# One semaphore per part of a weight unit, and matrix products with the upper part first

## Chip, cores and metric

The kernel runs on 1 core of one Trainium2 chip. The metric is the device time of one launch in microseconds (us); less is better. Three runs of the kernel before took 3330.92, 3332.18 and 3332.82 us; the median is 3332.18 us. TensorE is called PE below, VectorE DVE, ScalarE ACT, GpSimd POOL and SyncE SP.

## The reference

One inference step of a four-layer decoder, for a prompt of 512 tokens and 8 samples of 8 tokens: 576 tokens of width 1024. Layers 0 and 3 mix tokens with a gated MLP (gMLP), layer 1 with a convolution module, layer 2 with latent attention (MLA). Each layer ends in a SwiGLU of inner width 2816:

```
for i in range(DEPTH):                      # 4
    kind = i % 3                            # gMLP, convolution, MLA
    hp = xp * (1 + sc1p) + sh1p             # and the same for the samples
    op = gmlp_mixer(hp, ...) or conv_module(hp, ...) or mla(...)
    xp = layer_norm(ALPHA * xp + g1p * op, ln_mix_g[i], ln_mix_b[i])
    fp = (silu(h2 @ w_gate) * (h2 @ w_up)) @ w_down      # h2 = xp * (1 + sc2p) + sh2p
    xp = layer_norm(ALPHA * xp + g2p * fp, ln_ffn_g[i], ln_ffn_b[i])
```

All inputs are float32. The shifts, scales and gates come from a product of the condition vector with `ada_w`, 24 MB of weights for a layer.

## The kernel before

**Split operands.** Every weight and activation is split into an upper part (rounded to the matmul's reduced type, `w_hi`, `h_hi`, `a_hi`) and a lower part, the remainder (`w_lo`, `h_lo`, `a_lo`). For each block of 128 contracted values (an index k) PE computes three products into one PSUM bank: upper times upper, upper weight times lower activation, lower weight times upper activation.

**Units.** Weights come in units of up to 128 x 1024 values, 416 of them. There are five slots (`SLOTS`), unit u lies in slot u % 5. SP loads a unit into `w_raw`, which has the same memory as `w_lo` (`load_to`, L598), once PE has finished the last product with the unit five before it (a count of `acc_ready`). POOL makes `w_hi` from it (L717), then `w_lo` in place (L719), and counts up `split_full` once (`split_to`). SP also loads the `ada_w` blocks of 1 MB, in the same queue (L617).

**PE's order** is written out by hand. `take_units(k)` waits until the next k units are split as a whole, and hands out their slots. `half_product` is one unit of 128 output columns by one half of the tokens (288): 8 values of k, 24 matmuls (6 values of k and 18 matmuls in some units). In `gate_up` a step takes two units, one of the gate and one of the up matrix, and makes four such products. Each result is taken out of its bank by ACT and DVE, which then count up `acc_free`.

**After each LayerNorm** the next stage starts with `first_four`: four banks, first with k 0 to 3 (part 0), then with k 4 to 7 (part 1), since DVE delivers the lower part of the activations (`h_lo`, L2005) in quarters, counted by `h_ready`. In `first_halves` (gate_up and convolution) the four banks belong to four units, which are taken two at a time, at bank 0 and at bank 2; in `first_tokens` (gMLP and MLA) the activations are the stationary operand, and bank 2 takes the second pair of units. After bank 0 of part 1 PE makes the sums of the second token half for the LayerNorm, with `ones` as weights (`second_stats`; it waits for DVE's partial sums, L1947 and L1952, by `part_ready`); DVE and ACT then need them for the second half of `h_lo`, which the second call of `first_four` waits for.

**The matmuls of one product, before:**

```
for e, (w, a) in enumerate(((wh, ah), (wh, al), (wl, ah))):
    last = mm(out, lhsT, rhs, q == 0 and e == 0, q == n - 1 and e == 2)
```

The functions that the change touches, with what calls them:

Of the kernel before, what the change touches and what calls it, by code (L numbers as in the profile page):

```python
# [99 lines left out]
def trunk(nc, A, O):  # L100
    ctx = ExitStack()
    with ctx:
        def sem(name):
            return ctx.enter_context(nc.semaphore(name))
# [193 lines left out]
        act_c = sem("act_c")  # L298
        split_full = sem("split_full")
        acc_ready = sem("acc_ready")  # L300
# [408 lines left out]
        def _(pool):  # L709
            DG = Tally()  # L710

            def split_to(end):
                while U.n < end:
                    u = U.n
                    s, w = u % SLOTS, plan.words[u]
                    pool.wait_ge(raw_full[s], landed[u])
                    nc.gpsimd.tensor_scalar(w_hi[:, s, 0:w], w_raw[:, s, 0:w], 1.0, 1.0, ALU.mult, ALU.mult)  # L717
                    pool.drain()  # L718
                    nc.gpsimd.tensor_tensor(w_lo[:, s, 0:w], w_raw[:, s, 0:w], w_hi[:, s, 0:w].bitcast(F32),  # L719
                                            ALU.subtract).then_inc(split_full, 1)  # L720
                    U.up()
# [55 lines left out]
        def _(pe):  # L777
# [64 lines left out]
            def half_product(slot, kt, h, act, waits=None, a_waits=None):  # L842

                b = acc_bank()
                hi, lo = act
                if waits is not None or a_waits is not None:
                    for k in range(kt):
                        if k % 4 == 0 and a_waits is None:
                            pe.wait_ge(h_ready, 4 * waits + 2 * h + k // 4 + 1)
                        elif k % 4 == 0:  # L850
                            pe.wait_ge(a_ready, 8 + a_waits + 8 * h + k + 4)
                        for e, (w, a) in enumerate(((w_hi, hi), (w_hi, lo), (w_lo, hi))):
                            last = mm(pb[:, b, 0:HALF], w[:, slot, k * P:(k + 1) * P], a[:, k, half_cols(h)],
                                      k == 0 and e == 0, k == kt - 1 and e == 2)
# [15 lines left out]
            def late_product(s, kt, late):  # L870


                b = acc_bank()
                for k in range(kt):
                    if k in (0, kt - late):
                        pe.wait_ge(a_ready, 8 + AR.n - 2 * (late if k == 0 else 0))
                    for e, (w, a) in enumerate(((w_hi, a_hi), (w_hi, a_lo), (w_lo, a_hi))):
                        last = mm(pb[:, b, 0:HALF], w[:, s, k * P:(k + 1) * P], a[:, k, 0:HALF],
                                  k == 0 and e == 0, k == kt - 1 and e == 2)
                last.then_inc(acc_ready, 1)  # L880
                G.up()
# [39 lines left out]
            def first_four(t, h, step, units=None):  # L921
# [3 lines left out]
                for part_ in range(2):  # L925
                    pe.wait_ge(h_ready, 4 * t + 2 * h + part_ + 1)
                    for i in range(4):
                        if part_ == 0:
                            if units is not None and i % 2 == 0:
                                units(i // 2)  # L930
                            pe.wait_ge(acc_free, G.n + i + 1)
                        for k in range(4 * part_, 4 * part_ + 4):
                            last = step(i, k, (G.n + i) % BANKS)
                        if part_:
# [17 lines left out]
            def first_tokens(t, h, slots, widths):  # L952


                def step(i, k, b):
                    blk, tt = ((0, 2), (0, 3), (0, 4), (1, 2))[i] if h else divmod(i, 2)
                    n = widths[blk]
                    s, c = slots[blk][k // 4], slice(k % 4 * n, (k % 4 + 1) * n)
                    for e, (w, a) in enumerate(((w_hi, h_hi), (w_hi, h_lo), (w_lo, h_hi))):
                        last = mm(pb[:, b, 0:n], a[:, k, token_tile(tt)], w[:, s, c], k == 0 and e == 0,  # L960
                                  k == KT - 1 and e == 2)
                    return last

# [18 lines left out]
            def down_norm(kt, turn=False, by_half=False, late=0, between=None):  # L982

                slots = []
                if by_half and between is None:
                    for part_ in range(2):
                        pe.wait_ge(a_ready, 8 + AR.n - 16 + 4 * part_ + 4)
                        for i in range(4):
                            if part_ == 0:
                                slots += take_units(1)  # L990
                                pe.wait_ge(acc_free, G.n + i + 1)
                            for k in range(4 * part_, 4 * part_ + 4):
                                for e, (w, a) in enumerate(((w_hi, a_hi), (w_hi, a_lo), (w_lo, a_hi))):
                                    last = mm(pb[:, (G.n + i) % BANKS, 0:HALF], w[:, slots[i], k * P:(k + 1) * P],
                                              a[:, k, 0:HALF], k == 0 and e == 0, k == KT - 1 and e == 2)
                            if part_:
# [29 lines left out]
                b = acc_bank()  # L1026
                for k in range(kt):
                    for e, (w, a) in enumerate(((w_hi, a_hi), (w_hi, a_lo), (w_lo, a_hi))):
                        last = mm(pb[:, b, 0:HALF], w[:, slots[0], k * P:(k + 1) * P], a[:, k, half_cols(1)],
                                  k == 0 and e == 0, k == kt - 1 and e == 2)  # L1030
                    if k == kt // 2 - 1:
                        pe.wait_ge(part_ready, PT.n + 3)
# [1613 lines left out]
```

## Time and profile before

| quantity | value |
|---|---|
| median of three runs | 3332.18 us |
| the profiled execution's own time | 3332.91 us |
| its span | 3331.1 us |
| PE busy with matmuls | 3136.7 us (94%), 22524 matmuls |
| DVE busy | 1602.5 us (48%) |
| POOL busy | 1528.2 us (46%) |
| moved by DMA, mean | 104 GB/s |
| granted clock of PE, mean over the span | 0.974 |

The span runs from the first to the last instruction; the time of an execution is some 2 us more. A granted clock of 1.00 means 2.4 GHz for PE and 0.50 means 1.2 GHz. A matmul's row shows its length with what overlaps the next one, about 290 ns; the step from one start to the next is what counts. In a timeline the brackets at the end of a row give the idle time of the engine before it, and what ended it.

### The profile page before, as it was taken

To read this page: it belongs to the slowest core of one execution; us is meant where nothing else is said; L and a number is where in the kernel's file an instruction comes from. 1 tells how busy PE (TensorE), PEld (TensorE's weight loads), DVE (VectorE), ACT (ScalarE), POOL (GpSimd) and SP (SyncE) were. 2 spreads that over 40 slices of the span, in tenths; PEclk is the share of its full clock that TensorE was granted. 3 is DMA by queue.
4 is the path that set the end of the run, shared out by engine and by line. 5 is a ranking of instruction groups with operands and counts; after the bars stand their busy time and mean duration, and the time that the engine had idled before them with its cause. 6 is when DMAs were issued, how large, how long until landed. Compare 5 with 4: busy or idle time off the path is not lost.

```text
span 3331.1 us, 54036 instructions
## 1 busy us (share of the span) xinstructions
PE 3136.7 (94%) x22524; PEld 2898.7 (87%) x22524; DVE 1602.5 (48%) x2621; ACT 544.3 (16%) x1114; POOL 1528.2 (46%) x880
## 2 busy tenths in 40 slices
PE   6999999999899799999989888999999999899997
PEld 5999989999876589999986568999998999899997
DVE  3163563423688763424556536342353435634245
ACT  3120130000310240000233214000023201400002
POOL 2354445545467445455520044555553554455551
PEclk8999999999999899999989999999999999999998
DMA  5542344442221144433221324443222232122221
GB/s 218 213 119 72 111 173 129 140 130 80 80 64 39 31 170 128 152 126 96 79 69 43 109 79 152 133 152 118 89 77 71 79 95 80 58 83 83 83 85 52
DMA packets 450784, 344.83 MB, mean 104 GB/s; under 512 B 24953, under 2 KB 435953, under 8 KB 438238
## 3 DMA queue, kind: packets, MB, share of 16 engines
q1 hardware_dynamic: 441616, 323.89, 31.0%
q10 hardware_dynamic: 8925, 17.51, 1.5%
q8 instruction: 178, 2.92, 0.4%
q14 instruction: 65, 0.52, 0.0%
HBM read 336.81 MB, written 5.25 MB: 103 GB/s over the span
## 4 chain that ended last, share of the span: by engine, by line
issue 38%; POOL 24%; PE 19%; POOLq 11%; DVE 6%; DVEq 1%; ACT 1%; DMA 0%; ACTq 0%
POOL w_lo L719 24%; PE pb L789 18%; POOLq L718 11%; DVE pb L2263 2%; DVE pgT L2503 0%; DVE full L2247 0%; DVE yc L2272 0%; DVE xa L1978 0%; DVE att L2461 0%; DVE full L2249 0%; DVE pb L1971 0%; PE pb L866 0%; DMA out_y_prompt<-yo 0%; POOL a_lo L770 0%; DVEq L1977 0%
## 5 line engine op out<-in xcount | busy, mean ns | idle before, releaser
L717 POOL TENSOR_SCALAR w_hi<-w_raw 128x1024 fp32r<-128x1024 f32 (+2 forms) x416 | 448.4, 1078 | 1472.5 <-DMA w_raw<-in_ffn_w_up 423.1
L789 PE MATMUL pb<-h_hi,w_hi 128*128 128x288 f32 x3584 | 1074.0, 300 | 47.9 <-DVE h_lo L2005 21.8
L789 PE MATMUL pb<-h_lo,w_hi 128*128 128x288 f32 x3584 | 1061.7, 296 | 0.0
L789 PE MATMUL pb<-h_hi,w_lo 128*128 128x288 f32 x3584 | 1061.7, 296 | 0.0
L719 POOL TENSOR_TENSOR w_lo<-w_raw,w_hi 128x1024 fp32r<-128x1024 f32 (+2 forms) x416 | 985.1, 2368 | 62.1 <-issue 1.3
L789 PEld LDWEIGHTS pb<-h_hi,w_hi 128*128 128x128 f32 x3584 | 678.4, 189 | 102.0 <-issue 47.2
L789 PE MATMUL pb<-a_hi,w_hi 128*128 128x288 f32 x2176 | 652.3, 300 | 33.1 <-DVEq L2192 16.2
L789 PEld LDWEIGHTS pb<-h_lo,w_hi 128*128 128x128 f32 x3584 | 678.7, 189 | 0.3
L789 PEld LDWEIGHTS pb<-h_hi,w_lo 128*128 128x128 f32 x3584 | 678.5, 189 | 0.0
L789 PE MATMUL pb<-a_hi,w_lo 128*128 128x288 f32 x2176 | 646.4, 297 | 0.0
L789 PE MATMUL pb<-a_lo,w_hi 128*128 128x288 f32 x2176 | 646.3, 297 | 0.0
L789 PEld LDWEIGHTS pb<-a_hi,w_hi 128*128 128x128 f32 x2176 | 413.8, 190 | 41.7 <-DVEq L2192 17.1
L789 PEld LDWEIGHTS pb<-a_lo,w_hi 128*128 128x128 f32 x2176 | 413.5, 190 | 0.8
L789 PEld LDWEIGHTS pb<-a_hi,w_lo 128*128 128x128 f32 x2176 | 413.5, 190 | 0.0
L2079 DVE TENSOR_TENSOR pr<-pb,sg 128x288 f32<-128x288 f32 x176 | 80.2, 458 | 647.4 <-PE pb L789 646.7
L1553 ACT ACTIVATE sg<-pb 128x288 f32<-128x288 f32 x176 | 72.1, 411 | 1391.1 <-PE pb L789 1391.1
L1833 DVE TENSOR_TENSOR a_lo<-pr,a_hi 128x288 fp32r<-128x288 f32 x176 | 258.8, 1471 | 14.0 <-issue 1.1
L789 PE MATMUL pb<-w_hi,h_hi 128*128 128x256 f32 (+1 forms) x760 | 220.5, 290 | 28.9 <-DVE h_lo L2005 20.0
L1937 DVE SCALAR_TENSOR_TENSOR xa<-pb,gate,xa 128x288 f32<-128x288 f32 (+1 forms) x288 | 137.9, 480 | 208.5 <-PE pb L789 207.2
L789 PE MATMUL pb<-w_hi,h_lo 128*128 128x256 f32 (+1 forms) x760 | 217.4, 286 | 0.0
L789 PE MATMUL pb<-w_lo,h_hi 128*128 128x256 f32 (+1 forms) x760 | 217.1, 286 | 0.0
L789 PEld LDWEIGHTS pb<-w_hi,h_hi 128*128 128x128 f32 x760 | 148.7, 196 | 36.1 <-DVE h_lo L2005 21.7
(280 smaller groups left out, 2989.8 us busy)
## 6 DMA issues: line engine op xcount, KB each, us to landing
ada_w<-in_ada_w SPq DMA_DIRECT2D x88, 1024.0 KB, 5.8
w_raw<-in_ffn_w_gate SPq DMA_DIRECT2D x88, 512.0 KB, 4.5
w_raw<-in_ffn_w_up SPq DMA_DIRECT2D x88, 512.0 KB, 3.7
w_raw<-in_gmlp_w_in SPq DMA_DIRECT2D x64, 512.0 KB, 4.4
w_raw<-in_ffn_w_down SPq DMA_DIRECT2D x64, 512.0 KB, 4.0
w_raw<-in_gmlp_w_out SPq DMA_DIRECT2D x32, 512.0 KB, 4.2
w_raw<-in_ffn_w_down SPq DMA_DIRECT2D x32, 384.0 KB, 3.4
w_raw<-in_conv_w_pw SPq DMA_DIRECT2D x24, 512.0 KB, 3.9
```

The lines of the kernel that those rows point to most:

```text
L717: nc.gpsimd.tensor_scalar(w_hi[:, s, 0:w], w_raw[:, s, 0:w], 1.0, 1.0, ALU.mult, ALU.mult)
L718: pool.drain()
L719: nc.gpsimd.tensor_tensor(w_lo[:, s, 0:w], w_raw[:, s, 0:w], w_hi[:, s, 0:w].bitcast(F32), ALU.subtract).then_inc(split_full, 1)
L789: return nc.tensor.matmul(out, lhsT, rhs, start=start, stop=stop)
L1553: fn(sg[:, q, :], pb[:, b, 0:HALF], func, **kw).then_inc(sg_ready, 1)
L1833: return v.tensor_tensor(lo, src, hi.bitcast(F32), ALU.subtract)
L1937: last_ = v.scalar_tensor_tensor(out=y, in0=ps[:, 0:w], scalar=gp, in1=y, op0=ALU.mult, op1=ALU.add)
L2079: v.tensor_tensor(pr[:, q, :], pb[:, (G.n + 1) % BANKS, 0:HALF], sg[:, q, :], ALU.mult).then_inc(acc_free, 2)
L2263: v.scalar_tensor_tensor(out=own if k < CW - 1 else yp, in0=full[:, m % 3, k:k + SEQ], scalar=one(wdT, m, slice(k, k + 1)), in1=own, op0=A ...
```

## The change

POOL counts up `split_hi` when the upper part of a unit is written, and `split_lo` when the lower part is. `take_units` waits for nothing any more; PE waits for `split_hi` of a unit in front of the first matmul that reads its upper part, and for `split_lo` in front of the first that reads its lower part. In a product (or in a part of four values of k, where a product was cut before) the matmuls with the upper part come first, two for each k, and then those with the lower part, one for each k. The number of matmuls is the same, and so are the waits for activations and banks and the points at which products are reported as done.

```
-        split_full = sem("split_full")
+        split_hi = sem("split_hi")
+        split_lo = sem("split_lo")
...
                     pool.wait_ge(raw_full[s], landed[u])
-                    nc.gpsimd.tensor_scalar(w_hi[:, s, 0:w], w_raw[:, s, 0:w], 1.0, 1.0, ALU.mult, ALU.mult)
+                    nc.gpsimd.tensor_scalar(w_hi[:, s, 0:w], w_raw[:, s, 0:w], 1.0, 1.0, ALU.mult, ALU.mult
+                                            ).then_inc(split_hi, 1)
                     pool.drain()
                     nc.gpsimd.tensor_tensor(w_lo[:, s, 0:w], w_raw[:, s, 0:w], w_hi[:, s, 0:w].bitcast(F32),
-                                            ALU.subtract).then_inc(split_full, 1)
+                                            ALU.subtract).then_inc(split_lo, 1)
...
             def take_units(k):
-                pe.wait_ge(split_full, U.n + k)
                 slots = [(U.n + n) % SLOTS for n in range(k)]
+                for n, s in enumerate(slots):
+                    unit_in[s] = U.n + n
                 U.up(k)
                 return slots
+            unit_in = {}
+            HI, LO = Tally(), Tally()
+            def wait_hi(s):
+                if unit_in[s] >= HI.n:
+                    HI.up(unit_in[s] + 1 - HI.n)
+                    pe.wait_ge(split_hi, HI.n)
+            def wait_lo(s):
+                if unit_in[s] >= LO.n:
+                    LO.up(unit_in[s] + 1 - LO.n)
+                    pe.wait_ge(split_lo, LO.n)
...
             def product(out, ks, w_at, m_hi, m_lo, w_moves=False):
-                n = len(ks)
+                return part_product(out, ks, w_at, m_hi, m_lo, True, True, w_moves)
+            def part_product(out, ks, w_at, m_hi, m_lo, first, end, w_moves=False):
                 for q, k in enumerate(ks):
                     s, cols = w_at(k)
-                    wh, wl = w_hi[:, s, cols], w_lo[:, s, cols]
-                    ah, al = m_hi(k), m_lo(k)
-                    for e, (w, a) in enumerate(((wh, ah), (wh, al), (wl, ah))):
-                        lhsT, rhs = (a, w) if w_moves else (w, a)
-                        last = mm(out, lhsT, rhs, q == 0 and e == 0, q == n - 1 and e == 2)
+                    wait_hi(s)
+                    for e, a in enumerate((m_hi(k), m_lo(k))):
+                        lhsT, rhs = (a, w_hi[:, s, cols]) if w_moves else (w_hi[:, s, cols], a)
+                        mm(out, lhsT, rhs, first and q == 0 and e == 0, False)
+                for q, k in enumerate(ks):
+                    s, cols = w_at(k)
+                    wait_lo(s)
+                    lhsT, rhs = (m_hi(k), w_lo[:, s, cols]) if w_moves else (w_lo[:, s, cols], m_hi(k))
+                    last = mm(out, lhsT, rhs, False, end and q == len(ks) - 1)
                 return last
...
             def first_halves(t, h, slots):
-                def step(i, k, b):
-                    s, c = slots[i], slice(k * P, (k + 1) * P)
-                    for e, (w, a) in enumerate(((w_hi, h_hi), (w_hi, h_lo), (w_lo, h_hi))):
-                        last = mm(pb[:, b, 0:HALF], w[:, s, c], a[:, k, half_cols(h)], k == 0 and e == 0,
-                                  k == KT - 1 and e == 2)
-                    return last
+                def step(i, ks, b):
+                    return part_product(pb[:, b, 0:HALF], ks, lambda k: (slots[i], slice(k * P, (k + 1) * P)),
+                                        lambda k: h_hi[:, k, half_cols(h)], lambda k: h_lo[:, k, half_cols(h)],
+                                        0 in ks, KT - 1 in ks)
                 first_four(t, h, step, None if h else lambda _: slots.extend(take_units(2)))
...
```

The other places that had their own loop of three matmuls (`half_product`, `late_product`, `first_tokens`, `down_norm`) call `part_product` in the same way.

In the program before, PE, at the third bank of the very first `first_four` (layer 0, gMLP; `w_hi` and `w_lo` move, `h_hi` and `h_lo` are stationary, waits in brackets):

```order
L789 MATMUL pb<-w_hi,h_lo 128x256
L789 MATMUL pb<-w_lo,h_hi 128x256
L789 MATMUL pb<-w_hi,h_hi 128x256 [waits acc_free,split_full]
L789 MATMUL pb<-w_hi,h_lo 128x256
L789 MATMUL pb<-w_lo,h_hi 128x256
L789 MATMUL pb<-w_hi,h_hi 128x256
```

One wait for both units of the pair stands ahead of all matmuls of bank 2. At the same place in the program after, from the end of bank 1 through bank 2:

```order
L810 MATMUL pb<-w_lo,h_hi 128x256 x4
L810 MATMUL pb<-w_hi,h_hi 128x256 [waits split_hi,acc_free]
L810 MATMUL pb<-w_hi,h_lo 128x256
L810 MATMUL pb<-w_hi,h_hi 128x256
L810 MATMUL pb<-w_hi,h_lo 128x256
L810 MATMUL pb<-w_hi,h_hi 128x256
L810 MATMUL pb<-w_hi,h_lo 128x256
L810 MATMUL pb<-w_hi,h_hi 128x256
L810 MATMUL pb<-w_hi,h_lo 128x256
L810 MATMUL pb<-w_lo,h_hi 128x256 [waits split_lo]
L810 MATMUL pb<-w_lo,h_hi 128x256 x3
```

Bank 2 now begins behind a wait for the upper part of one unit, and its lower part is waited for eight matmuls later; the second unit of the pair is not asked for until part 1.

Before, PE, at the first step of `gate_up` behind the two calls of `first_four` (layer 0):

```order
L789 MATMUL pb<-h_hi,w_hi 128x288
L789 MATMUL pb<-h_lo,w_hi 128x288
L789 MATMUL pb<-h_hi,w_lo 128x288
L789 MATMUL pb<-h_hi,w_hi 128x288 [waits acc_free,split_full]
L789 MATMUL pb<-h_lo,w_hi 128x288
L789 MATMUL pb<-h_hi,w_lo 128x288
```

The wait in the fourth row is for two units, the gate's and the up matrix's. In the program after, further down in the same step, where the gate's product passes to its lower part and the up matrix's product begins:

```order
L810 MATMUL pb<-h_hi,w_hi 128x288
L810 MATMUL pb<-h_lo,w_hi 128x288
L810 MATMUL pb<-h_hi,w_lo 128x288 [waits split_lo]
L810 MATMUL pb<-h_hi,w_lo 128x288 x7
L810 MATMUL pb<-h_hi,w_hi 128x288 [waits split_hi,acc_free]
L810 MATMUL pb<-h_lo,w_hi 128x288
```

The gate's lower part is waited for behind 16 matmuls of its product, and the up matrix's unit behind all 24.

## Rows read from the trace of the kernel before

**Rows 1.** The page: span, and busy time of each engine.

```profile
span 3331.1 us, 54036 instructions
PE 3136.7 (94%) x22524; PEld 2898.7 (87%) x22524; DVE 1602.5 (48%) x2621; ACT 544.3 (16%) x1114; POOL 1528.2 (46%) x880
```

**Rows 2.** Waits of PE: line waited for, us in total, times, longest.

```profile
PE pb L789 <- POOL w_lo L719: 27.1, 14, 3.6
```

**Rows 3.** Timeline of PE: start, duration (us), instruction, count, idle before.

```profile
48.07 0.28 PE L789 MATMUL pb<-w_lo,h_hi 128*128 128x256 f32 x1
51.98 0.58 PE L789 MATMUL pb<-w_hi,h_hi 128*128 128x256 f32 x1 [3.64 <-POOL w_lo L719]
...
429.74 0.40 PE L789 MATMUL pb<-h_hi,w_hi 128*128 128x288 f32 x1 [1.43 <-POOL w_lo L719]
...
464.18 0.40 PE L789 MATMUL pb<-h_hi,w_hi 128*128 128x288 f32 x1 [2.67 <-POOL w_lo L719]
464.42 0.30 PE L789 MATMUL pb<-h_lo,w_hi 128*128 128x288 f32 x1
...
1031.01 0.40 PE L789 MATMUL pb<-h_hi,w_hi 128*128 128x288 f32 x1 [1.81 <-POOL w_lo L719]
...
1233.82 0.40 PE L789 MATMUL pb<-h_hi,w_hi 128*128 128x288 f32 x1 [2.80 <-POOL w_lo L719]
...
2061.82 0.61 PE L789 MATMUL pb<-h_hi,w_hi 128*128 128x288 f32 x1 [3.04 <-POOL w_lo L719]
...
2531.24 0.39 PE L789 MATMUL pb<-w_hi,h_hi 128*128 128x256 f32 x1 [0.27 <-POOL w_lo L719]
...
2899.11 0.40 PE L789 MATMUL pb<-h_hi,w_hi 128*128 128x288 f32 x1 [2.63 <-POOL w_lo L719]
```

**Rows 4.** Windows: length, busy (x matmuls) of PE, PEld, DVE, ACT, POOL; PEclk, DMA.

```profile
51.90:57.10 5.20, 5.12 (x24) 5.12 (x25) 4.55 (x4) 3.48 (x6) 3.59 (x3) 0.50 0.00 2
...
464.10:469.00 4.90, 4.82 (x36) 4.82 (x37) 0.65 (x2) 4.90 (x10) 0.03 (x1) 1.00 1.04 388
1234.80:1238.00 3.20, 3.20 (x15) 3.20 (x14) 0.00 (x0) 3.20 (x7) 0.00 (x0) 0.50 1.02 379
...
2061.80:2067.30 5.50, 5.47 (x23) 5.48 (x24) 0.60 (x2) 4.19 (x9) 0.00 (x0) 0.50 1.05 372
2900.50:2903.70 3.20, 3.20 (x15) 3.20 (x14) 0.00 (x0) 3.19 (x7) 3.19 (x2) 0.50 0.09 26
```

**Rows 5.** Timeline of POOL, at the start and at two places of layer 0.

```profile
44.94 2.38 POOL L719 TENSOR_TENSOR w_lo<-w_raw,w_hi 128x1024 fp32r<-128x1024 f32 x1
...
49.58 2.35 POOL L719 TENSOR_TENSOR w_lo<-w_raw,w_hi 128x1024 fp32r<-128x1024 f32 x1
...
427.31 2.37 POOL L719 TENSOR_TENSOR w_lo<-w_raw,w_hi 128x1024 fp32r<-128x1024 f32 x1
...
460.58 1.06 POOL L717 TENSOR_SCALAR w_hi<-w_raw 128x1024 fp32r<-128x1024 f32 x1 [26.01 <-DMA w_raw<-in_ffn_w_up]
461.78 2.35 POOL L719 TENSOR_TENSOR w_lo<-w_raw,w_hi 128x1024 fp32r<-128x1024 f32 x1
```

**Rows 6.** Windows: the longest stretch of PE without a stall (layer 3).

```profile
2955.25:3280.60 325.35, 325.35 (x2455) 325.35 (x2456) 1.00 0.28 82
```

**Rows 7.** Timeline of DVE at the start: second and third quarter of `h_lo`.

```profile
46.68 1.85 DVE L2005 TENSOR_TENSOR h_lo<-hf,h_hi 128x1152 fp32r<-128x1152 f32 x1 [2.79 <-ACT h_hi L1519]
...
53.74 3.11 DVE L2005 TENSOR_TENSOR h_lo<-hf,h_hi 128x1152 fp32r<-128x1152 f32 x1 [0.48 <-issue]
```

**Rows 8.** Windows: the convolution loop behind PE's stall at 1031.01.

```profile
1031.00:1060.00 29.00, 28.88 (x163) 22.77 (x164) 26.46 (x34) 2.37 (x4) 24.20 (x11) 1.00 0.13 38
```

**Rows 9.** Timeline behind LayerNorm (layer 0): DVE's sums, PE's sums, PE's next wait.

```profile
433.00 2.24 DVE L1952 TENSOR_REDUCE part<-sq 128x288 f32<-128x1152 f32 x1
...
434.58 2.10 PE L789 MATMUL pb<-part,ones 128*128 128x288 f32 x8
447.67 0.41 PE L789 MATMUL pb<-h_hi,w_hi 128*128 128x288 f32 x1 [2.68 <-DVE h_lo L2005]
```

More of the change, by code:

```diff
@@ L846, in half_product @@
                 if waits is not None or a_waits is not None:
-                    for k in range(kt):
-                        if k % 4 == 0 and a_waits is None:
+                    for k in range(0, kt, 4):
+                        if a_waits is None:
                             pe.wait_ge(h_ready, 4 * waits + 2 * h + k // 4 + 1)
-                        elif k % 4 == 0:
+                        else:
                             pe.wait_ge(a_ready, 8 + a_waits + 8 * h + k + 4)
-                        for e, (w, a) in enumerate(((w_hi, hi), (w_hi, lo), (w_lo, hi))):
-                            last = mm(pb[:, b, 0:HALF], w[:, slot, k * P:(k + 1) * P], a[:, k, half_cols(h)],
-                                      k == 0 and e == 0, k == kt - 1 and e == 2)
+                        last = part_product(pb[:, b, 0:HALF], range(k, min(k + 4, kt)),
+                                            lambda k: (slot, slice(k * P, (k + 1) * P)),
+                                            lambda k: hi[:, k, half_cols(h)], lambda k: lo[:, k, half_cols(h)],
+                                            k == 0, k + 4 >= kt)
                 else:
@@ L873, in late_product @@
                 b = acc_bank()
[L874 to L879, printed above, removed]
+                for k0, k1 in ((0, kt - late), (kt - late, kt)):
+                    pe.wait_ge(a_ready, 8 + AR.n - 2 * (kt - k1))
+                    last = part_product(pb[:, b, 0:HALF], range(k0, k1), lambda k: (s, slice(k * P, (k + 1) * P)),
+                                        lambda k: a_hi[:, k, 0:HALF], lambda k: a_lo[:, k, 0:HALF], k0 == 0, k1 == kt)
                 last.then_inc(acc_ready, 1)
@@ L931, in first_four @@
                             pe.wait_ge(acc_free, G.n + i + 1)
-                        for k in range(4 * part_, 4 * part_ + 4):
-                            last = step(i, k, (G.n + i) % BANKS)
+                        last = step(i, range(4 * part_, 4 * part_ + 4), (G.n + i) % BANKS)
                         if part_:
@@ L940, in first_halves, with step @@
             def first_halves(t, h, slots):
[L943 to L948 removed]
+                def step(i, ks, b):
+                    return part_product(pb[:, b, 0:HALF], ks, lambda k: (slots[i], slice(k * P, (k + 1) * P)),
+                                        lambda k: h_hi[:, k, half_cols(h)], lambda k: h_lo[:, k, half_cols(h)],
+                                        0 in ks, KT - 1 in ks)
                 first_four(t, h, step, None if h else lambda _: slots.extend(take_units(2)))
             def first_tokens(t, h, slots, widths):
[L955 removed]
+                def step(i, ks, b):
                     blk, tt = ((0, 2), (0, 3), (0, 4), (1, 2))[i] if h else divmod(i, 2)
                     n = widths[blk]
[L958 to L962, printed above, removed]
+                    return part_product(pb[:, b, 0:n], ks,
+                                        lambda k: (slots[blk][k // 4], slice(k % 4 * n, (k % 4 + 1) * n)),
+                                        lambda k: h_hi[:, k, token_tile(tt)], lambda k: h_lo[:, k, token_tile(tt)],
+                                        0 in ks, KT - 1 in ks, w_moves=True)
                 def units(blk):
@@ L991, in down_norm @@
                                 pe.wait_ge(acc_free, G.n + i + 1)
[L992 to L995, printed above, removed]
+                            last = part_product(pb[:, (G.n + i) % BANKS, 0:HALF], range(4 * part_, 4 * part_ + 4),
+                                                lambda k: (slots[i], slice(k * P, (k + 1) * P)),
+                                                lambda k: a_hi[:, k, 0:HALF], lambda k: a_lo[:, k, 0:HALF],
+                                                part_ == 0, part_ == 1)
                             if part_:
@@ L1026, in down_norm @@
                 b = acc_bank()
[L1027 to L1031, printed above, removed]
+                for k0, k1 in ((0, kt // 2), (kt // 2, kt)):
+                    last = part_product(pb[:, b, 0:HALF], range(k0, k1),
+                                        lambda k: (slots[0], slice(k * P, (k + 1) * P)),
+                                        lambda k: a_hi[:, k, half_cols(1)], lambda k: a_lo[:, k, half_cols(1)],
+                                        k0 == 0, k1 == kt)
+                    if k0 == 0:
                         pe.wait_ge(part_ready, PT.n + 3)
```

## The prediction

> **What bounds the kernel now.** I read the page first. PE is busy for 94% of the span, no other engine for more than half [rows 1], so nearly all time is matmuls, and the change removes none. What it can touch is PE's idle time, so the list of waits comes next: PE waited for POOL's `w_lo` 14 times, 27.1 us in all [rows 2]. The change cannot win more than this and what hangs on it. Then the timeline, for each of the 14. They are of two kinds [rows 3]:
>
> - Seven stand at bank 2 of the `first_four` behind a LayerNorm, all of 1.4 to 1.6 us like the one at 429.74 us.
> - Seven stand elsewhere: 3.64 us at the start (51.98), 2.67, 2.80, 3.04 and 2.63 us at the first ordinary step of `gate_up` in the four layers (464.18, 1233.82, 2061.82, 2899.11), 1.81 us in the convolution (1031.01) and 0.27 us in the last gMLP (2531.24).
>
> The windows behind the stalls come last, for the granted clock. Behind the stall at 51.98 PE runs at 0.50 (1.2 GHz), 24 matmuls in 5.20 us. Behind those at 1233.82, 2061.82 and 2899.11 it is at 0.50 too. Behind the one at 464.18 it stays at 1.00 (2.4 GHz) [rows 4].
>
> **Does the wait go, and what is late next?** At `gate_up` the old wait is for two units. The second one is late: POOL starts it at 460.58, has its upper part at 461.64 and its lower part at 464.13 [rows 5], and PE starts at 464.18 [rows 3]. After the change PE asks first for the gate's unit, which POOL finished long before (it was idle for 26.01 us ahead of 460.58). That product has 24 matmuls. An undisturbed matmul of 288 columns takes 325.35 / 2455 = 0.1325 us from start to start [rows 6], so the product takes 3.18 us, from about 461.4 to 464.5. By then both parts of the second unit are there. Nothing is late next: the stall goes whole. The other three have the same code and the same length.
>
> At the start, bank 2 needs both units of its pair now, the second one's lower part being ready at 49.58 + 2.35 = 51.93 us [rows 5]. After, its part 0 needs the first unit alone, ready at 44.94 + 2.38 = 47.32, before PE gets there (48.07 + 0.12). A matmul of 256 columns is an eighth shorter, 0.12 us, so part 0 ends at 48.2 + 24 x 0.12 = 51.1. Part 1 needs the second quarter of `h_lo`, there at 46.68 + 1.85 = 48.53, and takes 48 x 0.12 = 5.8 us, to 56.9. The second call needs the third quarter, there at 53.74 + 3.11 = 56.85 [rows 7]. So PE's whole lead fits, but only just: a later start than this would have been caught by DVE.
>
> **The terms.** A stall costs its idle time and about 0.15 us of the matmul that is running out: 51.98 - 48.07 - 0.12 = 3.79 for a row with 3.64 of idle [rows 3].
>
> - Start: 3.79 us of stall. Behind it 24 matmuls took 5.20 us instead of 24 x 0.12 = 2.88; I take 2.2 us, since the window is a little wider than they are [rows 4].
> - Layer 0, 464.18: 2.67 + 0.15 = 2.8 us; no clock term.
> - Layer 1, 1233.82: 2.95 us, and the half-speed window of 3.20 us. At 0.50 a matmul takes 5.50 / 23 = 0.239 us instead of 0.1325, so 45% of such time is lost: 1.4 us [rows 4].
> - Layer 2, 2061.82: 3.2 us, and 45% of 5.50 = 2.45 us.
> - Layer 3, 2899.11: 2.8 us, and 1.4 us.
> - Last gMLP, 2531.24: 0.4 us.
> - Convolution, 1031.01: 0. Its stall will go, but DVE is busy 26.46 of the next 29.00 us [rows 8]; it is what the loop waits for, and PE's lead is used up there. At most 1.9 us.
> - The seven behind LayerNorms: 0. At 429.74 POOL's last lower part had come at 427.31 + 2.37 = 429.68 [rows 5]; after, PE needs no more than the third unit and starts bank 2 at about 428.2, 1.6 us sooner. But `second_stats` then stands at 433.0 instead of 434.58 and needs DVE's last sum, which ends at 433.00 + 2.24 = 435.24 [rows 9]. Today PE spends these 0.7 us on the sums that it can already make, and is hardly late; then it will wait about 1.5 us. The stall moves by 5 us and comes back. The next wait (447.67, for `h_lo`) hangs on the same sum. At most 7 x 1.6 = 11 us.
>
> Stalls: 3.8 + 2.8 + 2.95 + 3.2 + 2.8 + 0.4 = 15.95 us. Clock: 2.2 + 1.4 + 2.45 + 1.4 = 7.45 us. Together 23.4 us.
>
> **What it adds.** PE has one wait per unit and part in place of one for each `take_units`: 826 matmuls with a split wait instead of 301, 525 more. Most are satisfied long before. What does a satisfied wait cost? The stretch without a stall has 102 products, each with a wait for its bank and every second one with a wait for a unit, and runs at 0.1325 us throughout [rows 6]. The steps between starts inside its products, 0.13 us, leave no room for a cost. The bound above is what a real stall leaves behind: the matmul after it starts 464.42 - 464.18 = 0.24 us later instead of 0.13, so 0.11 us x 525 = 58 us. I take 0, the value of the nearest rows, because those waits sit in the same kind of stream. The trace has no product whose lower parts follow each other; all three kinds of step (same weight, next weight, same activation) stand in that stretch at one pace, so the order of loads should not matter; 1% either way would be 30 us, and I see no reason for it. On POOL the upper part gets an increment; it waited 26 us here, and 0.05 us on 416 units would be hidden.
>
> [...]
>
> [...]
>
> **From the terms to the time.** 3332.91 - 23.4 = 3309.5 us against the profiled execution's own time. The median of the three runs is 0.7 us below it, so 3308.8; I say 3309.
>
> **The rivals.**
>
> 1. *The gain behind LayerNorms is real* (and the convolution's): 23.4 + 11 + 1.9 = 36 us, 3296. It needs DVE's sums to come sooner, and they don't hang on PE there. 7%.
> 2. *The clock takes part back.* The idle 1.5 us before the sums now lies nearer to the long wait for `h_lo`, and half-speed stretches can begin in layers where there are none. Each costs 1.4 to 2.5 us; with the 5.3 us of the clock terms in `gate_up` not won and up to two new stretches, the time is 3314 + 3 = 3317. For it: which stall is followed by half speed looks accidental. 23%.
> 3. *Slower: satisfied waits are not free* when they stand inside a product, in front of a load that would have been fetched ahead. 525 x 0.11 = 58 us less 23.4: 3367. It is slower than before from 0.045 us a wait on. Against it: the pace of the longest stretch [rows 6]. 5%.
> 4. *No change.* DMA is saturated behind the `gate_up` stalls (388 and 379 GB/s, share over 1.00 [rows 4]) so units land no sooner; if PE's lead only makes it wait for the next pair, or if new stalls of like size come up elsewhere, the time is 3326 to 3339. Against it: the next step, too, asks for its two units 3.2 us apart instead of both at its start, and the step in between takes four products, 12.7 us. 8%.
>
> My forecast, all seven stalls but the convolution's gone and the clock terms won within some 7 us, has the remaining 57%.
>
> **Range and chances.** 3298 holds all but the first rival and a lucky clock; 3323 holds the second rival; what lies outside is about two in ten. A difference of 0.2% (6.7 us) is about what a measurement of this kernel can tell from none. Faster by more: 57 + 7 + 23 = 87%. Within: 8%. Slower: 5%.
>
> **What will show it.** PE's list of waits has no lines of 2 to 3 us for `w_lo` or `w_hi` any more; the first `gate_up` step begins within 0.2 us of the last product. In layer 0 at the start PE runs from 44 to about 63 us without a stall, with the clock at 1.00 from 47 on. `part,ones` rows now have an idle time of 1 to 2 us with DVE's L1952 as releaser, seven times, and the wait for `h_lo` is as long as before. DVE's and POOL's busy times are unchanged, and the 288-column step is 0.1325 us. The forecast is wrong if that step has grown, if PE waits for a DMA or `w_hi` in the second step of `gate_up`, or if the share of half-speed time is not smaller by about 17 us.

## The result, and the profile after

| | before | after |
|---|---|---|
| median, 5 runs each | 3332.22 us | 3314.64 us |
| lowest to highest | 3330.92 to 3335.33 | 3313.22 to 3320.63 |
| the profiled execution's own time | 3332.91 us | 3313.4 us |

The ratio is 0.9948, with a 95% interval of 0.9933 to 0.9963: faster by 0.5%. The forecast was 3309 us with a range of 3298 to 3323. The time lies inside the range, 5.6 us above the point.

The page of the profile after, span and busy times, beside [rows 1]:

```profile
span 3311.6 us, 54131 instructions
PE 3124.5 (94%) x22524; PEld 2885.8 (87%) x22524; DVE 1635.9 (49%) x2621; ACT 544.2 (16%) x1114; POOL 1530.1 (46%) x880
```

PE's busy time fell by 12.2 us with the same number of matmuls; fewer of them ran at half speed. DVE's rose by 33.4 us with the same number of instructions, of which `a_lo` makes 28.9 (258.8 to 287.7 us) and the rounding to `a_hi` 5.4 (128.9 to 134.3): something slows DVE down, which the prediction did not have. It had DVE's busy time unchanged.

PE's waits after (engine, line, what it waited for: us in total, times, longest). Lines of stages that did not change are left out:

```profile
PE pb L810 <- DVE h_lo L2032: 44.0, 12, 8.1
...
PE pb L810 <- DVEq L1980: 14.7, 14, 5.3
...
PE pb L810 <- DVE a_lo L1860: 6.6, 6, 1.2
...
PE pb L810 <- DVE bst L2142: 2.1, 1, 2.1
PE pb L810 <- POOL w_lo L721: 2.0, 2, 1.1
```

Of the 27.1 us for `w_lo` [rows 2] 2.0 are left. Four lines took some of it: L1980, DVE's sums behind LayerNorms (7.9 us in 9 waits before), `a_lo` (one wait before, six now), `bst`, which is new, and `h_lo` (41.8 us in 11 waits before).

Four of the places of [rows 3], in the timeline of PE after. None has an idle time in brackets:

```profile
1224.66 0.29 PE L810 MATMUL pb<-h_hi,w_hi 128*128 128x288 f32 x1
...
2047.71 0.29 PE L810 MATMUL pb<-h_hi,w_hi 128*128 128x288 f32 x1
...
2515.26 0.29 PE L810 MATMUL pb<-w_hi,h_hi 128*128 128x256 f32 x1
...
2878.68 0.29 PE L810 MATMUL pb<-h_hi,w_hi 128*128 128x288 f32 x1
```

The windows behind three of them, beside the third, the fourth and the last of [rows 4] (length; busy time and count of PE, PEld, DVE, ACT, POOL; granted clock; DMA share; GB/s):

```profile
1224.60:1230.10 5.50, 5.50 (x44) 5.50 (x43) 3.15 (x3) 5.50 (x12) 2.77 (x2) 1.00 1.02 429
2047.70:2053.20 5.50, 5.50 (x44) 5.50 (x43) 3.26 (x3) 5.50 (x12) 2.83 (x2) 1.00 1.01 423
2878.60:2884.10 5.50, 5.50 (x44) 5.50 (x44) 3.78 (x3) 5.50 (x12) 5.06 (x4) 1.00 0.83 246
```

The clock stays at 1.00 (2.4 GHz): 44 matmuls in the 5.50 us in which 23 ran before.

In layer 0, POOL's rows for the unit that PE had waited for, beside the last two of [rows 5]:

```profile
456.95 1.05 POOL L718 TENSOR_SCALAR w_hi<-w_raw 128x1024 fp32r<-128x1024 f32 x1 [26.19 <-DMA w_raw<-in_ffn_w_up]
458.17 2.50 POOL L721 TENSOR_TENSOR w_lo<-w_raw,w_hi 128x1024 fp32r<-128x1024 f32 x1 [0.16 <-issue]
```

PE works through the gate's product meanwhile, from 457.27 to 460.4, and has the lower part (ready at 460.67) some 2 us before it asks for it, 16 matmuls into the next product. A stretch without a stall, beside [rows 6]:

```profile
3077.00:3222.00 145.00, 145.00 (x1097) 145.00 (x1096) 50.33 (x76) 6.37 (x16) 78.58 (x45) 1.00 0.27 81
```

145.00 / 1097 = 0.1322 us for a step, as before (0.1325).

**A ledger of the lead.** Both programs have the same 22524 matmuls, so the start of the n-th one before, less its start after, says what has been won up to there. Between two steps this lead stays level within some 0.05 us. Each line is the difference of the levels on its two sides, worked out from the two traces:

```
place (start us before)             step of the lead   forecast
start, up to 57.1                   +5.0
start, 63.0: PE waits for a bank    -2.3               net 6.0, measured 2.7
gate_up layer 0, 464.2              +2.92              2.8
gate_up layer 1, 1233.8 and clock   +3.06 +1.54        2.95 +1.4
gate_up layer 2, 2061.8 and clock   +3.19 +2.68        3.2 +2.45
gate_up layer 3, 2899.1 and clock   +2.89 +1.54        2.8 +1.4
last gMLP, 2531                     +0.53              0.4
convolution, 1031.0 to 1136         +2.07 -2.10        0
seven LayerNorms                    +12.15 -10.68      0
five starts of down products        -6.94              not in it
all else, steps of up to 2.2        +4.2               0
end                                 +19.8              23.4
```

Three places make 4.6 us of "all else" (at 252, 1721 and 2802 us before): there PE ran at half speed for 6.8, 13.7 and 6.8 us in the profile before and for 3.4, 6.8 and 3.4 us in that after. In the second profile of the kernel before it was 6.8, 10.2 and 3.4 us, so this part varies from one execution to the next.

**The start.** PE's timeline after, at bank 2 of the first `first_four`, and where its second call begins to need a bank again:

```profile
49.13 0.41 PE L810 MATMUL pb<-w_hi,h_hi 128*128 128x256 f32 x1
...
57.46 0.64 PE L810 MATMUL pb<-w_lo,h_hi 128*128 128x256 f32 x4
60.20 0.36 PE L810 MATMUL pb<-w_hi,h_hi 128*128 128x256 f32 x1 [2.10 <-DVE bst L2142]
```

DVE at the same time, which answers to [rows 7]:

```profile
53.74 3.15 DVE L2032 TENSOR_TENSOR h_lo<-hf,h_hi 128x1152 fp32r<-128x1152 f32 x1 [0.48 <-issue]
56.99 0.43 DVE L2020 TENSOR_TENSOR hf<-xa,cs 128x256 f32<-128x256 f32 x1
57.49 0.42 DVE L2020 TENSOR_TENSOR hf<-hf,cb 128x256 f32<-128x256 f32 x1
57.99 0.29 DVE L2030 CAST h_hi<-hf 128x256 fp32r<-128x256 f32 x1
58.36 1.36 DVE L2032 TENSOR_TENSOR h_lo<-hf,h_hi 128x1152 fp32r<-128x1152 f32 x1
59.63 1.40 DVE L2142 BATCH_NORM_STATS2 bst<-v_sb 128x6 f32<-128x256 f32 x4
```

Bank 2 starts at 49.13, not at 51.98. PE still ran at half speed then (the third figure from the right is its granted clock):

```profile
43.70:49.60 5.90, 5.75 (x27) 5.76 (x28) 3.01 (x3) 5.90 (x13) 5.57 (x4) 0.51 0.03 9
```

Before, half speed ended at 46.9 us, after at 49.5, which cost about 1 us of the lead. In other profiles it ended at 48.3 (before) and at 49.0 and 48.4 us (after), so this differs by execution. Then, behind its products (here at 60.20) PE needs a free bank, and DVE frees it in its statistics (`bst`), which stand in DVE's queue behind the last quarter of the split. PE arrives earlier and waits for the same thing.

**A LayerNorm** (layer 0), the place of [rows 9]: PE, then DVE.

```profile
428.96 1.13 PE L810 MATMUL pb<-part,ones 128*128 128x288 f32 x4
431.34 1.24 PE L810 MATMUL pb<-part,ones 128*128 128x288 f32 x4 [1.24 <-DVEq L1980]
...
443.57 0.40 PE L810 MATMUL pb<-h_hi,w_hi 128*128 128x288 f32 x1 [2.69 <-DVE h_lo L2032]
```

```profile
429.12 2.13 DVE L1979 TENSOR_REDUCE part<-sq 128x288 f32<-128x1152 f32 x1
```

DVE's sum ends at 429.12 + 2.13 = 431.25, and PE takes it at 431.34, after 1.24 us of idle. The wait for `h_lo` is 2.69 us, before it was 2.68. From the end of PE's sums to the end of this wait it is 443.57 - 432.58 = 10.99 us; before it was 447.67 - 436.68 = 10.99 [rows 9].

**The start of a down product** (layer 0). In the profile after, PE, DVE and POOL:

```profile
829.79 0.41 PE L810 MATMUL pb<-a_hi,w_hi 128*128 128x288 f32 x1 [1.12 <-DVE a_lo L1860]
```

```profile
826.16 0.90 DVE L1858 CAST a_hi<-pr 128x288 fp32r<-128x288 f32 x1
827.13 2.61 DVE L1860 TENSOR_TENSOR a_lo<-pr,a_hi 128x288 fp32r<-128x288 f32 x1
```

```profile
825.84 1.05 POOL L718 TENSOR_SCALAR w_hi<-w_raw 128x1024 fp32r<-128x1024 f32 x1 [5.41 <-DMA w_raw<-in_ffn_w_down]
827.05 2.37 POOL L721 TENSOR_TENSOR w_lo<-w_raw,w_hi 128x1024 fp32r<-128x1024 f32 x1 [0.16 <-issue]
```

In the profile before, DVE and POOL at the same place:

```profile
833.38 0.31 DVE L1831 CAST a_hi<-pr 128x288 fp32r<-128x288 f32 x1
833.76 0.46 DVE L1833 TENSOR_TENSOR a_lo<-pr,a_hi 128x288 fp32r<-128x288 f32 x1
```

```profile
833.83 1.30 POOL L717 TENSOR_SCALAR w_hi<-w_raw 128x1024 fp32r<-128x1024 f32 x1 [5.76 <-DMA w_raw<-in_ffn_w_down]
835.28 2.40 POOL L719 TENSOR_TENSOR w_lo<-w_raw,w_hi 128x1024 fp32r<-128x1024 f32 x1
```

The same instruction, `a_lo`, takes 0.46 us before and 2.61 us after. After, POOL's subtraction had begun 0.08 us ahead of it and ended at 829.42; `a_lo` ended at 829.74, 0.32 us later. All 92 `a_lo` of this kind that began within a subtraction of POOL end 0.31 to 0.32 us after it; before the change these were 73. So DVE did not run slower, it stood until POOL was done. Before, the order at this place was the reverse: `a_lo` had begun 0.07 us ahead of POOL's rounding, and the rounding took 1.30 us in place of 1.05. The Trainium skill, page "SBUF — State Buffer" ("Who interferes with whom"), has this rule: a DVE instruction with two inputs in SBUF and a GpSimd instruction that reads SBUF exclude each other, and whichever issues first blocks the other to its end. The trace agrees with it. The rounding to `a_hi` just ahead stood as well: begun within POOL's rounding it took 0.90 us in place of 0.31.

POOL comes sooner because the units land sooner after SP's issue (issues: count, KB, median us to landing). Before, and then after:

```profile
w_raw<-in_ffn_w_down SPq DMA_DIRECT2D x64, 512.0 KB, 4.0
w_raw<-in_gmlp_w_out SPq DMA_DIRECT2D x32, 512.0 KB, 4.2
```

```profile
w_raw<-in_ffn_w_down SPq DMA_DIRECT2D x64, 512.0 KB, 3.4
w_raw<-in_gmlp_w_out SPq DMA_DIRECT2D x32, 512.0 KB, 3.6
```

### The profile page after: what moved, and what is told of

Read it like the earlier page. It is cut to its first block, busy times and chain, and to the rows that moved or that the text cites. A ratio compares the mean times of both kernels' runs of the same rounds, so it can differ in the third digit from the quotient of the medians.

```text
span 3311.6 us, 54131 instructions
## 1 busy us (share of the span) xinstructions
PE 3124.5 (94%) x22524; PEld 2885.8 (87%) x22524; DVE 1635.9 (49%) x2621; ACT 544.2 (16%) x1114; POOL 1530.1 (46%) x880
## 3 DMA queue, kind: packets, MB, share of 16 engines
HBM read 336.81 MB, written 5.25 MB: 103 GB/s over the span
## 4 chain that ended last, share of the span: by engine, by line
PE 33%; issue 29%; POOL 18%; POOLq 8%; DVE 8%; ACT 1%; DVEq 1%; DMA 0%; ACTq 0%
PE pb L810 32%; POOL w_lo L721 18%; POOLq L720 8%; DVE pb L2290 2%; DVE pb L1998 1%; DVE h_lo L2032 0%; DVE pgT L2530 0%; DVE xa L2005 0%; ACT hf L1546 0%; ACT h_hi L1546 0%; DVEq L1980 0%; DVEq L2004 0%; DVE part L1979 0%; DVE a_lo L1860 0%; DVE full L2274 0%
## 5 line engine op out<-in xcount | busy, mean ns | idle before, releaser
L718 POOL TENSOR_SCALAR w_hi<-w_raw 128x1024 fp32r<-128x1024 f32 (+2 forms) x416 | 450.3, 1083 | 1443.5 <-DMA w_raw<-in_ffn_w_up 405.1
L810 PE MATMUL pb<-h_hi,w_hi 128*128 128x288 f32 x3584 | 978.9, 299 | 28.4 <-DVE h_lo L2032 22.5
L810 PE MATMUL pb<-h_lo,w_hi 128*128 128x288 f32 x3584 | 967.3, 295 | 0.0
L810 PE MATMUL pb<-a_hi,w_hi 128*128 128x288 f32 x2176 | 599.6, 300 | 38.3 <-DVEq L2219 16.2
L810 PE MATMUL pb<-a_lo,w_hi 128*128 128x288 f32 x2176 | 593.2, 297 | 0.0
L810 PE MATMUL pb<-h_hi,w_lo 128*128 128x288 f32 x3584 | 555.7, 295 | 2.0 <-POOL w_lo L721 2.0
L810 PEld LDWEIGHTS pb<-h_hi,w_lo 128*128 128x128 f32 x3584 | 503.9, 188 | 2.5 <-POOL w_lo L721 2.5
L810 PE MATMUL pb<-a_hi,w_lo 128*128 128x288 f32 x2176 | 341.4, 296 | 0.0
L810 PEld LDWEIGHTS pb<-a_hi,w_lo 128*128 128x128 f32 x2176 | 307.5, 189 | 0.0
L1860 DVE TENSOR_TENSOR a_lo<-pr,a_hi 128x288 fp32r<-128x288 f32 x176 | 287.7, 1635 | 14.0 <-issue 1.1
L1963 DVE TENSOR_TENSOR pb<-pb,gate 128x64 f32<-128x64 f32 x144 | 33.4, 232 | 276.6 <-PE pb L810 275.4
```

The lines of the kernel that those rows point to most:

```text
L1860: return v.tensor_tensor(lo, src, hi.bitcast(F32), ALU.subtract)
L1963: v.tensor_tensor(bt(ps[:, HP:HALF]), bt(ps[:, HP:HALF]), gs, ALU.mult)
```

## The experiments

Eleven runs were made beside the first two. The kernel before took 3329.89, 3330.75 and 3331.26 us (medians) beside the three groups below.

### The two kernels themselves again

Both unchanged. **The kernel before:**

> The kernel before, once more, with a profile from the same chip and minutes as the kernels beside it. In the profile of the changed kernel the units of ffn_w_down and gmlp_w_out land in 3.4 and 3.6 us (median), in that of before in 4.0 and 4.2; and DVE's lower part a_lo, at the last step of gate_up, is overlapped by POOL's w_lo and takes 2.6 us instead of 0.46 to 1.3, with a stall of PE of 1.3 to 1.5 us behind it, at six of those places instead of one. Theory A (the landing is a matter of chip, run or placement and not of the change): this run shows the shorter landings and more than one such stall, and the time is within 0.3% of before. Theory B (the change itself makes them land sooner): this run shows 4.0 and 4.2 us and one stall again.

Measured: 3330.14 us, ratio 1.0002 (0.9992 to 1.0011). The units land in 4.0 and 4.2 us and PE waits once for `a_lo`, so theory B holds.

**The kernel after:**

> The changed kernel, once more, on the same chip as the others of this call: 0.993 to 0.996 of before. Does it show again six stalls of 1.3 to 1.5 us at the start of the down products, and half speed of PE at the same places? If the clock is accident, half-speed time differs by some 10 us between its two profiles; if it follows from the program's timing, by less than 4 us.

Measured: 3314.32 us, ratio 0.9956 (0.9940 to 0.9973). The landing of 3.3 us against 4.0, the six waits for `a_lo` against one, and the clock at the `gate_up` steps are there again, so they belong to the change and not to one execution. The total time at half speed does not: 173.3 and 156.8 us in two profiles of before, 134.1 and 140.9 us in two of after. The 6.8 us between the last two lie between the two marks set for it (4 and 10 us), so they decide nothing.

### One half of the change alone: the lazy wait

```
-                    for e, a in enumerate((m_hi(k), m_lo(k))):
+                    for e, (w, a) in enumerate(((wh, m_hi(k)), (wh, m_lo(k)), (wl, m_hi(k)))):
...
-                    pe.wait_ge(split_hi, HI.n)
+                    pe.wait_ge(split_lo, HI.n)
```

> One part of the change alone: one semaphore per unit as before, counted up when both parts are there, but waited for in front of the first matmul that reads the unit, and not in pairs; the three matmuls of each k stay together. Theory 1 (what held PE up was the second unit of the pair, not the lower part): the stalls of 2.6 to 3.0 us at gate_up and the one of 3.6 us at the start are gone here as well, and the time equals that of the whole change within 0.1%. Theory 2 (the upper part first is what wins): at least half of the gain is missing, 3324 us or more.

Measured: 3317.86 us, ratio 0.9969 (0.9957 to 0.9980). PE's waits for `w_lo` and `a_lo`:

```profile
PE pb L808 <- DVE a_lo L1854: 6.0, 6, 1.1
...
PE pb L808 <- POOL w_lo L719: 4.4, 3, 2.2
```

To wait for each unit where it is first read brings some 12 of the 16 us, and also what goes against it: the landings of 3.3 us and the six waits for `a_lo`. The stalls at `gate_up` and at the start are gone, as in theory 1, and theory 2 is out. The interval overlaps that of the whole change, but all seven runs (3316.76 us and more) lie above all four of it beside them (up to 3315.61). Part of the difference is seen: at 892.6 and 2851.1 us PE waits 2.04 and 2.20 us for the whole unit, where the changed kernel waits 0.95 and 1.08 us for its lower part.

### The other half alone: upper part first

```
             def take_units(k):
+                pe.wait_ge(split_lo, U.n + k)
...
-                    pe.wait_ge(split_hi, HI.n)
...
-                    pe.wait_ge(split_lo, LO.n)
```

> The other part alone: upper parts first in each product, but one semaphore per unit, waited for in pairs as before. By theory 1 nothing changes: all 14 stalls for w_lo are there, with 26 to 28 us, and the time is within 0.2% of before; the step between matmuls of 288 columns stays at 0.1325 us. By theory 2 the order helps by itself: it is below 3325 us. If the new order of loads cost anything, the time would be above 3339 us.

Measured: 3330.54 us, ratio 0.9998 (0.9988 to 1.0008). PE's wait is that of [rows 2]:

```profile
PE pb L807 <- POOL w_lo L719: 26.5, 14, 3.4
```

The order of the matmuls is worth nothing as long as the wait is for the whole pair. It also costs nothing: with the loads in the new sequence the time is the same within 0.1%.

### POOL held back at the start of the down products

```
+            hold, made = {}, 8
+            for l in range(DEPTH):
+                made += 32 if l % 3 == 0 else 16
+                for first, count in GU:
+                    made += 2 * count
+                    hold[plan.mark[l, "m", first + count - 1] + 3] = made
...
                     pool.wait_ge(raw_full[s], landed[u])
+                    if u in hold:
+                        pool.wait_ge(a_ready, hold[u])
```

> The changed kernel, in which POOL, before it splits the unit three ahead of the first unit of each of the 12 starts of down products, waits until DVE has made the finished gate_up results' pairs (a_hi and a_lo). Theory 1: the six stalls of PE for a_lo (0.99 to 1.39 us each in the changed kernel, one in the kernel before) come from POOL's w_lo subtraction running beside DVE's a_lo; they vanish, no wait for w_lo takes their place, since POOL has three units in hand, and the time falls by 5 to 7 us, to about 3308 us. Theory 2: a_lo is slow for another reason (DVE's reads of PSUM, the earlier landing of transfers); the stalls stay and the time is that of the changed kernel, 3314 us. Theory 3: POOL, held back by 2 us at each place, delivers later and PE waits for w_lo or w_hi: 3314 us or more.

Measured: 3309.05 us, ratio 0.9934 (0.9920 to 0.9947). At the place shown above, DVE and POOL:

```profile
827.57 0.46 DVE L1868 TENSOR_TENSOR a_lo<-pr,a_hi 128x288 fp32r<-128x288 f32 x1
```

```profile
828.18 1.05 POOL L726 TENSOR_SCALAR w_hi<-w_raw 128x1024 fp32r<-128x1024 f32 x1 [6.68 <-DVE a_lo L1868]
829.40 2.40 POOL L729 TENSOR_TENSOR w_lo<-w_raw,w_hi 128x1024 fp32r<-128x1024 f32 x1 [0.16 <-issue]
```

All six waits are gone and none for POOL has come. Theory 1 holds: the median is 5.3 us below that of the changed kernel's repeat (3314.32), and none of its five runs (up to 3312.12) reaches the lowest there (3312.85). Between the traces the lead grows by 8.15 us at the six places; 4.3 us of it went again elsewhere; in this profile half speed lasts 155.2 us in all, in the changed kernel's 134.1.

### DVE empties the first banks earlier

```
+            firsts = (gmlp_first, conv_first, mla_first)
             for g in range(2):
                 samples(0, g)
                 halves(1, g)
-            firsts = (gmlp_first, conv_first, mla_first)
-            firsts[0]()
+                if g == 0:
+                    firsts[0]()
```

> The changed kernel, in which DVE, at the very start, empties the four PSUM banks of the first products between the two halves of the first transfers' splits, instead of after all of them. Theory 1: PE's 2.38 us stall at 60.20 us, in which it waits for a free bank, goes, since the lead of 5 us that PE has by its 159th matmul is no longer taken back there: about 2 us less than the changed kernel, 3312 us. Theory 2: the split of the last quarter of the activations comes later in its place and PE waits for h_lo as long: 3314 us.

Measured: 3312.10 us, ratio 0.9945 (0.9931 to 0.9958). The row that stood at 60.20 with 2.10 us of idle:

```profile
57.13 0.35 PE L810 MATMUL pb<-w_hi,h_hi 128*128 128x256 f32 x1 [0.34 <-DVE bst L2142]
```

The stall is gone in the trace. The gain of some 2 us is of the size expected, but its interval overlaps that of the changed kernel.

### The LayerNorm's sums one bank later

```
-                            if t and h == 0 and i == 0:
+                            if t and h == 0 and i == 1:
```

> The changed kernel, in which PE issues the LayerNorm's second sums after the second bank of the second half, not after its first, at eight places. Theory 1 (the prediction's): the seven places are bound by DVE; the 1.3 us that PE now idles in front of the sums vanish, and its wait for DVE's h_lo or the one behind the sums grows as much or more, since the sums themselves come some 3 us later: 3314 us or up to 8 times 1.5 us more. Theory 2: the gain of 1.6 us at each place was real and only lost by the place of the sums: up to 9 us less, 3305 us.

Measured: 3322.02 us, ratio 0.9975 (0.9966 to 0.9984), some 7 us more than the changed kernel. In layer 0:

```profile
430.88 2.14 PE L810 MATMUL pb<-part,ones 128*128 128x288 f32 x8
...
444.00 0.40 PE L810 MATMUL pb<-h_hi,w_hi 128*128 128x288 f32 x1 [4.26 <-DVE h_lo L2032]
```

The sums run in one piece, without the idle 1.24 us, and the wait for `h_lo` grows from 2.69 to 4.26 us. It ends 10.98 us after the sums, as in both kernels above. So the stall behind a LayerNorm is DVE's, wherever PE spends it, and the gain of 1.6 us ahead of it can't be kept in this way.

### A wait before every k

```
                 if unit_in[s] >= HI.n:
                     HI.up(unit_in[s] + 1 - HI.n)
-                    pe.wait_ge(split_hi, HI.n)
+                pe.wait_ge(split_hi, HI.n)
...
-                    pe.wait_ge(split_lo, LO.n)
+                pe.wait_ge(split_lo, LO.n)
```

> The changed kernel, in which PE waits for the unit's upper and lower part in front of every k, not only in front of the unit's first read: 6598 waits for each part in place of 413, nearly all of them satisfied long before. Theory 1: a satisfied wait costs PE nothing, since its queue runs ahead of the array: 3314 us, and steps of 132.5 ns as before. Theory 2: one costs 0.11 us, as one event instruction of the queue does: up to 12370 times 0.11, some 1300 us more. Theory 3: part is hidden; the steps of 256 or 288 columns grow by what isn't.

Measured: 3314.84 us, ratio 0.9950 (0.9936 to 0.9964). The window of [rows 6], of the same length:

```profile
2941.00:3266.35 325.35, 325.35 (x2459) 325.35 (x2458) 127.55 (x182) 16.45 (x35) 176.71 (x103) 1.00 0.28 82
```

A step is 325.35 / 2459 = 0.1323 us; before it was 0.1325. Of the 13196 waits for units 12306 ride on a weight load; the events of PE's queue grew only from 712 to 1085. Some 12370 satisfied waits changed the time by less than the runs differ.

### Both mends together

The edits of the two mends above, in one kernel.

> The changed kernel with both mends: POOL waits for the finished a_hi and a_lo at the 12 starts of down products, and DVE empties the first four banks between the two halves of the first transfers. If the two losses are independent, their gains add: 3314.3 less 5.5 less 2 is about 3307 us, with neither the stall of 2.4 to 2.7 us at 57 to 60 us nor those of 1.0 to 1.6 us for a_lo. If one gain was an accident of the clock, 3309 us or more.

Measured: **3303.79 us**, ratio 0.9919 (0.9905 to 0.9932). It is the fastest of all here. Its page begins:

```profile
span 3300.2 us, 54143 instructions
PE 3119.7 (95%) x22524; PEld 2882.2 (87%) x22524; DVE 1589.1 (48%) x2621; ACT 544.2 (16%) x1114; POOL 1529.6 (46%) x880
```

It is 3 us below the 3307 that was expected of the two together. In the ledger against the changed kernel's profile the six `a_lo` places give 8.2 us and the start 2.1; the rest of the 11.3 is the balance of steps both ways, most of them at places with half speed.

**The same two on the lazy wait alone:**

> The same two mends on the kernel with one semaphore, waited for where a unit is first read, and the matmuls in the order of the kernel before. If the two parts' own semaphores and the order are worth only what was measured without the mends (3317.9 against 3314.3), it takes some 3.5 us more than with them: about 3310.5 us. If they are worth nothing, both kernels take the same, 3307 us.

Measured: 3308.67 us, ratio 0.9928 (0.9915 to 0.9942). With the mends the separate semaphores and the order made 4.9 us, without them 3.5; both times the two intervals overlap.

**The changed kernel beside them:**

> The changed kernel itself once more, beside the two mended ones on the same chip: 3314 us, with six stalls for a_lo and one at 60 us.

Measured: 3315.77 us, ratio 0.9955 (0.9941 to 0.9968). On this chip the two mends took 12.0 us off it.

## Why the prediction came out as it did

**Right: the stalls at `gate_up`.** Forecast 11.75 us of stalls and 5.25 us of clock; the ledger has 12.06 and 5.76.

**Right: the clock goes with the stall.** The prediction gave 23% to its second rival, in which the clock takes part back, since the 2.63 us stall in layer 3 was followed by half speed and the 2.67 us one in layer 0 was not. All profiles together say more: behind the four `gate_up` places the three profiles with the stalls (before, twice, and upper part first alone) show half speed in 10 of 12 cases, and the ten profiles without them in none of 40. The second rival is wrong for these places. The length of the stall alone does not say which is followed by half speed: at these places one of 2.40 us was and one of 3.01 us was not. The rival had looked at another place as well, the wait of 2.7 us for `h_lo` behind a LayerNorm, and there it is half right. In layer 0 half speed follows this wait in none of the three profiles with the stalls, and in six of nine without them (the later sums, which lengthen it, left out); in layer 1 in three of three, and two of nine; in layer 2 in one of three, and four of nine. New stretches begin and others end: 4 of 12 cases with the stalls, 12 of 27 without, which is no clear difference. The half-speed time of one kernel varies from profile to profile: 134.1, 140.9 and 144.8 us in three of the changed kernel.

**Right: no gain behind LayerNorms and in the convolution.** The ledger has +1.7 to +1.8 and -1.5 to -1.8 us at five of seven; at 889.68 and 2847.96 us PE now waits 0.95 and 1.08 us for `w_lo` in the middle of a product, and keeps 0.5 and 0.35 us. In sum 1.5 us were kept where 0 was said. The later sums (3322 us) show that the wait is DVE's. In the convolution 2.07 us came and 2.10 went.

**Right: satisfied waits cost nothing**, against the third rival (0.11 us each), by the experiment with a wait before every k; and the pace of a stretch with lower parts in a row is that of before.

**Wrong, the failed step: the start.** The prediction said: "So PE's whole lead fits, but only just". It had looked for the next thing that PE asks for in `h_ready` alone. The next wait for a bank (`acc_free`), which the second call makes too, was left out. DVE frees that bank behind the fourth quarter of the split, which ends at 58.36 + 1.36 = 59.72, 2.8 us after the third. PE was ahead by 5.0 us at 57 us and lost 2.3 of it at 60.20. The other 1.0 us was missing before: the prediction had the clock at 1.00 from 47 us on, and it was at 0.50 until 49.5. The term was 6.0 us and measured 2.7. With the bank emptied earlier the stall goes. (A matmul of 256 columns is a ninth shorter than one of 288, not an eighth; the 0.12 us that the sum used is the step that the trace has.)

**Missing: what POOL, once sooner, collides with.** The prediction costed the change on POOL at nothing, as an increment on 416 units, and POOL's own busy time did hardly change (1528.2 and 1530.1 us). It did not ask what else in the program lies beside POOL's subtraction. At five starts of down products it now lies over DVE's `a_lo`: -6.94 us. The run with POOL held back shows that this is the cause. The shorter landing that moves POOL is a result of the lazy wait (it is there without the new order, and the new order alone does not bring it). Why it shortens stays open: the transfers have as many packets (about 1040 in a unit of the down matrix), of the same length, 27 ns. The median packet starts 2.1 us after the issue, before it was 2.2, and the last one 3.1, before 3.7. With a wait before every k, which is a change on PE alone, the landing is 3.7 us and PE waits for `a_lo` four times.

**The sum.** 23.4 - 3.3 (start) + 0.8 (`gate_up`) + 0.1 (last gMLP) - 6.9 (`a_lo`) + 1.5 (LayerNorms) + 4.2 (all else) = 19.8 us, the lead at the end; the convolution comes out at 0. The two misses make 10.2 us; small gains that were not forecast gave back 6.6 of them. The largest of these, the 4.2 us, comes from half-speed stretches that vary between executions. That the time came so near to the point is in this part luck. The other 2 us between forecast and result are the distance of the medians from the two profiled executions: 0.7 us below before, 1.2 us above after. The prediction's mark "half-speed time smaller by about 17 us" came out as 39 us in the first pair of profiles and 16 us in the second; one profile each cannot measure it.

## What to carry to other kernels

When a wait is made later or finer, follow the lead that it gives to each of the semaphores that the engine asks for next (operand, bank, slot), and not only to the one that was late before. Ask what the engine that is not on the critical path will now lie beside: here a subtraction of POOL that came about 1 us sooner cost as much as a third of the gain, and one wait that holds it back in 12 places won 5 us back. A per-unit wait at the first read is what pays when units are taken in pairs (some 12 of 16 us). The order of the products alone brought nothing; together with one semaphore for each part it seems to add 3 to 5 us, which the intervals don't settle.

## What the runs showed of the hardware

- DVE's `a_lo` subtraction of 128x288, both inputs in SBUF, takes 0.46 us alone; begun within POOL's subtraction it ends 0.31 to 0.32 us after that one's end, 92 times out of 92, up to 2.65 us in all. Begun within POOL's rounding (L718) it ends 0.30 to 0.31 us after that, 18 times out of 18.
- Some 12000 added waits that are satisfied, in front of matmuls in a full stream, did not change a step of 0.132 us.
- Half speed (1.2 GHz) followed the stalls of 2.4 to 3.0 us at three of the `gate_up` places in all three profiles that had them. At the fourth, in layer 0, it followed one of 2.67 us and not the two of 2.67 and 3.01 us. Where these stalls were gone it came in none of 40 cases.
